# An encoder kernel in split fp32: the last three steps of each down product by tiles, and projections, seam and end reordered

## The chip, the cores and the metric

The kernel runs on one core of one Trainium2 chip. The metric is the device time of one execution in microseconds (us), first to last instruction and what lies around them. A core has TensorE (PE, matmuls into eight PSUM banks), VectorE (DVE), ScalarE (ACT), GpSimd (POOL), and SyncE (SP), which here only issues transfers. Each engine runs its own instruction list in order and waits on semaphores for the others.

## What is computed

Two independent sequences (x_prompt and x_sample) of 1024 tokens and 1024 channels go through the same layer, all in float32:

```python
h = rmsnorm(x, norm_mix)
z = h @ w_in
a = pool_mixer(z[..., :512]) @ w_up_pool          # means over 2, 4, 8, 16 tokens, small maps
b = attention_branch(z[..., 512:]) @ w_up_attn    # 12 heads, three dilated windows, merged
gates = sigmoid(h @ w_gate + b_gate)
x = x + (g_a * a + g_b * b) @ w_out
h = rmsnorm(x, norm_ffn)
x = x + (silu(h @ w_ffn_gate) * (h @ w_ffn_up)) @ w_ffn_down   # 2816 hidden channels
y = rmsnorm(x, norm_final)
```

## The kernel before

**Split operands.** Each float32 operand is held as a high part (rounded by ACT) and a low part (the rest, subtracted by POOL or DVE). A product is three matmuls: high by high, high by low, low by high (`three`, L1089 to L1093). A group of three matmuls of 128x512 is the unit of TensorE's work here.

**Seven products in place of eight.** The large products are done by a Strassen-Winograd scheme of seven products on half-size blocks, with sums and differences of the blocks formed by POOL.

**The down product.** The last large product of a sequence (hidden activations by `w_ffn_down`) is seven down products, numbered o = 0 to 6 (`DOWN`, L59). Each is KC = 11 steps (k = 0 to 10), and each step takes one 128-row piece of the contraction. In a step TensorE does four groups, one for each tile t = 0 to 3 of 128 tokens; each tile has its own PSUM bank (`down_products`, L1357). So a down product is 44 groups, and the four banks are complete one after another in its last step. Products use bank group 0 or 1 in turn; products 0, 1, 5 and 6 begin with cleared banks and the others go on adding.

For a step with index m the other engines make two operands.

- ACT rounds the activations (`part_hi`, L1672, tile d_hi) and then the weights (`operand_hi`, L1461, tile t_hi). It does both for step m + 4 after step m of TensorE is done, since there are four slots of each (RING = 4). "Step done" is the semaphore `prod_done`, which the last matmul of tile t = 3 raises.
- DVE subtracts d_lo (`part_low`, L2132).
- POOL subtracts t_lo (`low_part`, L836). In products 1, 2 and 4 POOL first forms the weights' difference for the next step, and in product 5 it forms, behind t_lo, the difference for product 6 (`rows_sum`, L956, L977): two POOL instructions a step, where products 0, 3 and 6 have one.
- SP loads the activations from DRAM (d_rows) and the weights (w_ffn_down).

DVE then adds the four banks into X, the residual (`add_quarter`, L2139), at the first step of the next product. The results of product 4 are added twice, the second time at (5, 1). Where steps are written (o, k), o is the down product and k its step.

**The seam.** While sequence 0 is in its down products, the first normalisation of sequence 1 is made in between: SP loads the tokens after step (3, 0), ACT makes their statistics (`first_stats`, at (2, 10), (3, 2), (5, 1), (6, 9)), DVE normalises (`first_norm`, at (3, 0), (3, 2), (3, 5), (3, 7), (5, 4), (5, 6), and two at (6, 10)), and POOL forms four sums for each pair p of token tiles (`mix_s1` to `mix_s4`, one at each place of `SUMS_AT`, L136). In product 6 TensorE transposes the parts between its steps (`part_transposes`, `EARLY`, L131), ACT and DVE copy them out, and ACT and DVE also make the final norm of the first four tiles of sequence 0 (`final_stats`, `final_norm`), which SP stores. Behind those stores SP loads the last tokens and the first weights of sequence 1.

**Up and out projections.** Before the up projections DVE splits the four pooled operands (`mix_low`, L2080), the fourth behind the loop over the front products, so behind `after_product` of the last gate product (L1929, which writes gst when SP's earlier store of it has landed). The up projections (`up_products`) fill banks 4r to 4r + 3 for channel block j, r = j mod 2, and DVE multiplies the gates in (`gated`, L2087, L2094). Then `out_products` (L1336) does 24 visits in three rounds; a visit adds one 128-row block of `w_out` into the banks of two or three token tiles. Visit 0 takes tiles 0, 1, 2, that is banks 0 to 5, and banks 4 and 5 are those that the gates of block j = 7 are read from.

**The end.** In sequence 1 DVE adds the four tiles of product 6, ACT makes the statistics of the last four tiles, DVE normalises them, and ACT issues their four stores, behind all four statistics (`store_out`, L1690).

## Time and profile before

| what | us |
|---|---|
| median of three runs | 2621.22 (2619.81 to 2622.74) |
| the profiled execution, its own time | 2620.28 |
| its span, first to last instruction | 2618.5 |
| TensorE busy | 2543.1 (97% of the span), 12048 matmuls |
| POOL, DVE, ACT busy | 1874.5, 1221.4, 1051.9 |
| mean granted clock of TensorE | 0.995 |

A busy time is the union of an engine's instructions. Matmuls are pipelined, so their records overlap, and a step in which TensorE waits a little for each operand can still look fully busy: the length of a product is read from the starts of its first matmuls, not from the busy share. "Idle" in a row is the time that the engine stood before that instruction, with what released it. A row of the view of stretches gives start and end, the length, then for PE, PEld (weight loads), DVE, ACT and POOL the busy time and, in brackets, the count of instructions, then TensorE's granted clock as a share of full speed, the DMA share and GB/s; the stretches below run from the first matmul of one down product to the first of the next. A row of the timeline gives start, length, engine, line, operation, tiles and shapes.

### The profile page before, as it was taken

How to read it: one execution, taken by the hardware profiler on the slowest of the kernel's cores; microseconds unless marked ns; L12 is line 12 of the kernel's file. 1: busy time of each engine (PE TensorE's matmuls, PEld its weight loads, DVE VectorE, ACT ScalarE, POOL GpSimd, SP SyncE). 2: the span in 40 equal slices, each digit the busy share in tenths (PEclk: the TensorE clock that was granted, in tenths of full speed). 3: DMA queues.
4: the chain of work that ended last, by engine and by line, in shares of the span. 5: the costliest groups of instructions: out<-in, count | busy, mean ns of one | idle time of the engine just before them, and what ended most of it. 6: DMA issues, size and time to landing. Idle time of an engine off the chain costs nothing. (4 is left out here: it accounts for less than half of the span.)

```text
span 2618.5 us, 33338 instructions
## 1 busy us (share of the span) xinstructions
PE 2543.1 (97%) x12048; PEld 2065.2 (79%) x12048; DVE 1221.4 (47%) x1673; ACT 1051.9 (40%) x2034; POOL 1874.5 (72%) x1376
## 2 busy tenths in 40 slices
PE   6999999999999999998989999999999999999998
PEld 5887777778888888876778877777878888888786
DVE  6753556644322222354677535566443222223545
ACT  5224554444433233344552345544444333233444
POOL 7775456545888888797977754465468888887985
PEclk8999999999999999999999999999999999999999
DMA  3444455462233333463444435554623333335534
GB/s 130 128 131 125 144 158 175 143 243 77 81 108 97 116 98 97 157 206 120 141 141 124 149 107 154 152 175 161 229 81 92 97 99 107 101 105 165 181 122 140
DMA packets 331858, 350.76 MB, mean 134 GB/s; under 512 B 30640, under 2 KB 242992, under 8 KB 330160
## 3 DMA queue, kind: packets, MB, share of 16 engines
q1 hardware_dynamic: 329392, 342.23, 41.6%
q10 hardware_dynamic: 2304, 6.40, 0.7%
q8 instruction: 98, 1.61, 0.3%
q14 instruction: 64, 0.52, 0.1%
HBM read 249.28 MB, written 99.29 MB: 133 GB/s over the span
## 5 line engine op out<-in xcount | busy, mean ns | idle before, releaser
L1091 PE MATMUL ps<-S,t_hi 128*128 128x512 f32 (+2 forms) x2336 | 917.1, 393 | 9.1 <-POOL t_lo L841 6.3
L1093 PE MATMUL ps<-S,t_lo 128*128 128x512 f32 (+2 forms) x2336 | 903.7, 387 | 0.0
L1092 PE MATMUL ps<-S,t_hi 128*128 128x512 f32 (+2 forms) x2336 | 903.0, 387 | 0.0
L1091 PEld LDWEIGHTS ps<-S,t_hi 128*128 128x128 f32 x2336 | 438.7, 188 | 110.3 <-issue 12.7
L1093 PEld LDWEIGHTS ps<-S,t_lo 128*128 128x128 f32 x2336 | 438.6, 188 | 89.9
L1092 PEld LDWEIGHTS ps<-S,t_hi 128*128 128x128 f32 x2336 | 439.1, 188 | 84.1
L841 POOL TENSOR_TENSOR t_lo<-wraw,t_hi 128x512 fp32r<-128x512 f32 x185 | 246.4, 1332 | 205.8 <-ACT t_hi L1489 203.4
L841 POOL TENSOR_TENSOR t_lo<-wraw_ff,t_hi 128x512 fp32r<-128x512 f32 x225 | 293.9, 1307 | 93.4 <-ACT t_hi L1489 89.3
L1489 ACT CAST t_hi<-wraw_ff 128x512 fp32r<-128x512 f32 x225 | 139.6, 623 | 366.8 <-PE ps L1093 366.6
L2136 DVE TENSOR_TENSOR d_lo<-d_raw,d_hi 128x512 fp32r<-128x512 f32 x154 | 178.9, 1164 | 207.0 <-ACT d_hi L1680 206.4
L841 POOL TENSOR_TENSOR t_lo<-R,t_hi 128x512 fp32r<-128x512 f32 x154 | 233.1, 1519 | 46.5 <-ACT t_hi L1489 46.5
L1091 PE MATMUL ps<-t_hi,d_hi 128*128 128x512 f32 x616 | 248.7, 404 | 11.8 <-POOL t_lo L841 11.8
L1092 PE MATMUL ps<-t_lo,d_hi 128*128 128x512 f32 x616 | 241.1, 391 | 0.0
L1093 PE MATMUL ps<-t_hi,d_lo 128*128 128x512 f32 x616 | 241.1, 391 | 0.0
L1489 ACT CAST t_hi<-wraw 128x512 fp32r<-128x512 f32 x185 | 115.2, 623 | 303.7 <-PE ps L1093 299.0
L1919 DVE TENSOR_TENSOR u<-u,ps 128x512 f32<-128x512 f32 x82 | 56.3, 686 | 255.8 <-PE ps L1093 255.8
L841 POOL TENSOR_TENSOR t_lo<-t,t_hi 128x512 fp32r<-128x512 f32 x74 | 101.7, 1374 | 98.6 <-ACT t_hi L1489 98.3
L1091 PEld LDWEIGHTS ps<-t_hi,d_hi 128*128 128x128 f32 x616 | 116.3, 189 | 54.8 <-POOL t_lo L841 32.3
L1680 ACT CAST d_hi<-d_raw 128x512 fp32r<-128x512 f32 x154 | 95.3, 619 | 137.0 <-PE ps L1093 93.7
L995 POOL TENSOR_TENSOR wo_lo<-wo_raw,wo_hi 128x1024 fp32r<-128x1024 f32 x32 | 82.5, 2582 | 91.8 <-ACT wo_hi L1646 91.8
L1922 DVE TENSOR_TENSOR v<-u,ps 128x512 f32<-128x512 f32 x82 | 56.4, 687 | 195.8 <-PE ps L1093 195.7
L1489 ACT CAST t_hi<-R 128x512 fp32r<-128x512 f32 x154 | 95.3, 619 | 116.5 <-POOL R L977 101.8
(169 smaller groups left out, 4054.6 us busy)
## 6 DMA issues: line engine op xcount, KB each, us to landing
d_raw<-d_rows SPq DMA_DIRECT2D x154, 256.0 KB, 3.2
d_rows<-act_f SPq DMA_DIRECT2D x110, 256.0 KB, 2.1
wraw_ff<-w_ffn_up SPq DMA_DIRECT2D x44, 512.0 KB, 4.7
R<-w_ffn_down SPq DMA_DIRECT2D x88, 256.0 KB, 3.1
wraw<-w_in SPq DMA_DIRECT2D x42, 512.0 KB, 5.6
sp_rows<-gst SPq DMA_DIRECT2D x80, 256.0 KB, 2.5
wraw_ff<-w_ffn_gate SPq DMA_DIRECT2D x40, 512.0 KB, 5.0
wo_raw<-w_out SPq DMA_DIRECT2D x36, 512.0 KB, 3.3
```

The costliest lines, as they stand in the source:

```text
L841: nc.gpsimd.tensor_tensor(shape(t_lo[r][:, :]), src, shape(t_hi[r][:, :]).bitcast(F32), ALU.subtract).then_inc(t_ready, 1)
L995: nc.gpsimd.tensor_tensor(wo_lo[r][:, :], wo_raw[op % 2][:, :], wo_hi[r][:, :].bitcast(F32), ALU.subtract).then_inc(wo_ready, 1)
L1091: nc.tensor.matmul(o_ps, w[0], r[0], start=begins, stop=False, skip_group_check=True)
L1092: nc.tensor.matmul(o_ps, w[0], r[1], start=False, stop=False, skip_group_check=True)
L1093: return nc.tensor.matmul(o_ps, w[1], r[0], start=False, stop=ends, skip_group_check=True)
L1489: nc.scalar.copy(dst, src).then_inc(thi_ready, 1)
L1680: nc.scalar.copy(d_hi[d % 4][:, :], d_raw[d % 4][:, :]).then_inc(dhi_ready, 1)
L1919: V_.tensor_tensor(u, u, b1, ALU.add).then_inc(sums_done, 1)
L1922: V_.tensor_tensor(v1[:, :], u, b2, ALU.add).then_inc(sums_done, 1)
L2136: V_.tensor_tensor(d_lo[d % 4][:, :], d_raw[d % 4][:, :], d_hi[d % 4][:, :].bitcast(F32), ALU.subtract).then_inc(d_ready, 1)
```

## The change

Four parts, with the diff below.

- **Tail.** In every down product but product 6 of sequence 0, TensorE does steps 0 to 7 as before and then goes tile by tile: steps 8, 9, 10 for tile 0, then for tiles 1, 2 and 3. The order of the 44 groups changes, not their number. DVE adds tiles 0 to 2 at step 8 of the same product and tile 3 at step 0 of the next.
- **Seam.** The sums, statistics and norms for sequence 1 sit at other steps: the second pair's sums all in product 6, the third pair's statistics, norms and sums later in product 6, with its last two sums behind POOL's last down step. The four final norms of product 6 sit one step later.
- **Projections.** The fourth `mix_low` goes ahead of the last `after_product`. `out_products` takes tiles 0 and 1 of visits 0 and 1 first, and then tile 2 of both.
- **End.** In sequence 1 DVE adds tiles 0 and 1, normalises, adds tile 2, normalises, adds tile 3, and normalises twice. SP issues all eight stores of sequence 1, each when its tile is ready.

```diff
@@ -120,6 +120,8 @@
         VISITS.append((_r, _k, _op))
 N_WO = len(SLOT_OF)
 
+FIRST_VISITS = ((0, (0, 1)), (1, (0, 1)), (0, (2,)), (1, (2,)))
+
 N2_AFTER = {8 + v: [v - 1] for v in range(1, 8)}
 N2_AFTER.update({17: [7, 8], 18: [9, 10], 19: [11, 12], 20: [13, 14]})
 
@@ -133,7 +135,11 @@
 EARLY_DONE = 21
 
 
-SUMS_AT = ((3, 3), (3, 4), (3, 5), (3, 6), (3, 8), (3, 9), (6, 0), (6, 1), (6, 5), (6, 6), (6, 7), (6, 8))
+
+SUMS_AT = ((3, 6), (3, 7), (3, 8), (3, 9), (6, 0), (6, 1), (6, 2), (6, 3), (6, 9), (6, 10))
+
+
+TAIL = 3
 
 
 
@@ -781,7 +787,7 @@
                     if m == N_PROD + 3 * KC and s + 1 < SEQS:
                         sp.wait_ge(prod_done, due("prod_done", s, N_PROD))
                         first_tokens(s + 1)
-                for n in range(2 if s + 1 < SEQS else 4):
+                for n in range(2 if s + 1 < SEQS else TT):
                     store_out(s, n)
 
 
@@ -1068,6 +1074,8 @@
                             mix_s3(s + 1, 0, p)
                         else:
                             mix_s4(s + 1, 0, p)
+                    if s + 1 < SEQS and m == N_OPS - 1:
+                        mix_last(s + 1, 0, 2)
                     i = FF_PAIRS // 2 - 1
                     if m == N_PROD + 3:
                         first_sums(s, i)
@@ -1354,14 +1362,14 @@
                 if v < 7 and t == OUT_ROUNDS[rnd][0][-1]:
                     ins.then_inc(wo_used, 1)
 
-            def down_products(s, m):
+            def down_products(s, m, ts=range(4)):
 
                 o, k = divmod(m - N_PROD, KC)
                 part, group, begins, _ = DOWN[o]
                 pe.wait_ge(t_ready, due("t_ready", s, m + 1))
                 pe.wait_ge(d_ready, due("d_ready", s, m - N_PROD + 1))
                 slot, d = slot_of(m), (m - N_PROD) % 4
-                for t in range(4):
+                for t in ts:
                     b = 4 * group + t
                     if k == 0:
                         bank_read(b)
@@ -1393,7 +1401,9 @@
                     pair_banks(s, n)
                 for j, a in UP_ORDER:
                     up_products(s, j, a)
-                for visit in range(len(VISITS) - 3):
+                for visit, tiles in FIRST_VISITS:
+                    out_products(s, visit, tiles)
+                for visit in range(2, len(VISITS) - 3):
                     out_products(s, visit, OUT_ROUNDS[visit // 8][0])
                     part_transposes(s, 1, N2_AFTER.get(visit, ()))
                 for t in OUT_ROUNDS[-1][0]:
@@ -1405,11 +1415,17 @@
                     for m in range(7 * n + (4 if n == FF0 else 0), 7 * n + 7):
                         pair_product(s, m)
                     pair_banks(s, n)
-                for m in range(N_PROD, N_OPS):
-                    down_products(s, m)
-                    o, k = divmod(m - N_PROD, KC)
-                    if o == 6 and s + 1 < SEQS:
-                        part_transposes(s + 1, 0, EARLY.get(k, ()))
+                for o in range(len(DOWN)):
+                    first = N_PROD + KC * o
+                    seam = o == 6 and s + 1 < SEQS
+                    for k in range(KC if seam else KC - TAIL):
+                        down_products(s, first + k)
+                        if seam:
+                            part_transposes(s + 1, 0, EARLY.get(k, ()))
+                    if not seam:
+                        for t in range(4):
+                            for k in range(KC - TAIL, KC):
+                                down_products(s, first + k, (t,))
 
         @block.scalar
         def _(act):
@@ -1824,12 +1840,12 @@
                     if o == 2 and k == 0:
                         act.wait_ge(ff_stored[0], due("ff_stored0", s, 36))
                         act.dma_start(g_fin[:, :], norm_final.partition_broadcast(P)).then_inc(gfin_in, 16)
-                    if s + 1 < SEQS and (o, k) in ((2, 10), (3, 2), (5, 1)):
-                        first_stats(s + 1, ((2, 10), (3, 2), (5, 1)).index((o, k)))
+                    if s + 1 < SEQS and (o, k) in ((2, 10), (3, 2), (6, 0)):
+                        first_stats(s + 1, ((2, 10), (3, 2), (6, 0)).index((o, k)))
                     if o == 6 and s + 1 < SEQS:
                         part_his(s + 1, 0, EARLY.get(k - 1, ()))
-                    if o == 6 and k in (1, 2, 5, 6):
-                        final_stats(s, (1, 2, 5, 6).index(k))
+                    if o == 6 and k in (2, 3, 6, 7):
+                        final_stats(s, (2, 3, 6, 7).index(k))
                     if o == 6 and k == 9 and s + 1 < SEQS:
                         first_stats(s + 1, 3)
                 if s + 1 < SEQS:
@@ -1837,8 +1853,6 @@
                 else:
                     for n in range(4, TT):
                         final_stats(s, n)
-                    for n in range(4, TT):
-                        store_out(s, n)
 
             for q in range(4):
                 act.wait_ge(tiles_stored[q], due(f"tiles_stored{q}", SEQS, 0))
@@ -2136,11 +2150,11 @@
                 V_.tensor_tensor(d_lo[d % 4][:, :], d_raw[d % 4][:, :], d_hi[d % 4][:, :].bitcast(F32), ALU.subtract
                                  ).then_inc(d_ready, 1)
 
-            def add_quarter(s, o, which):
+            def add_quarter(s, o, which, ts=range(4)):
 
                 _, group, _, quarters = DOWN[o]
                 h, n = quarters[which]
-                for t in range(4):
+                for t in ts:
                     if t == 3:
                         dve.wait_ge(prod_done, due("prod_done", s, N_PROD + KC * (o + 1)))
                     else:
@@ -2171,6 +2185,8 @@
                 dve.wait_ge(const_in, 16 * 4)
 
                 for m in range(FRONT + 1):
+                    if m == FRONT:
+                        mix_low(s, 3)
                     if m:
                         after_product(s, m - 1)
                     n, o = divmod(m - 1, 7)
@@ -2202,7 +2218,6 @@
                         merge_step(s, 2 * (m - SPREAD0 - 1) + 1)
                     if MERGE0 + 12 <= m < MERGE0 + 15:
                         mix_low(s, m - MERGE0 - 12)
-                mix_low(s, 3)
                 merged_low(s, 0)
                 merged_low(s, 1)
                 for j in range(TT):
@@ -2239,17 +2254,19 @@
                 for m in range(N_PROD, N_OPS):
                     o, k = divmod(m - N_PROD, KC)
                     if k == 0 and o:
-                        add_quarter(s, o - 1, 0)
+                        add_quarter(s, o - 1, 0, (3,))
+                    if k == KC - TAIL and o < 6:
+                        add_quarter(s, o, 0, range(3))
                     if k == 1 and o == 5:
                         add_quarter(s, o - 1, 1)
                     if m + 4 < N_OPS:
                         part_low(s, m + 4)
                     if o == 6 and k == 2:
                         dve.wait_ge(gfin_in, due("gfin_in", s, 1))
-                    if s + 1 < SEQS and (o, k) in ((3, 0), (3, 2), (3, 5), (3, 7), (5, 4), (5, 6)):
-                        first_norm(s + 1, ((3, 0), (3, 2), (3, 5), (3, 7), (5, 4), (5, 6)).index((o, k)))
-                    if o == 6 and k in (2, 3, 6, 7):
-                        final_norm(s, (2, 3, 6, 7).index(k))
+                    if s + 1 < SEQS and (o, k) in ((3, 0), (3, 1), (3, 4), (3, 6), (6, 1), (6, 2)):
+                        first_norm(s + 1, ((3, 0), (3, 1), (3, 4), (3, 6), (6, 1), (6, 2)).index((o, k)))
+                    if o == 6 and k in (3, 4, 7, 8):
+                        final_norm(s, (3, 4, 7, 8).index(k))
                     if o == 6 and s + 1 < SEQS:
                         part_los(s + 1, 0, EARLY.get(k - 1, ()))
                     if o == 6 and k == 10 and s + 1 < SEQS:
@@ -2257,15 +2274,18 @@
                         first_norm(s + 1, 7)
                 if s + 1 < SEQS:
                     part_los(s + 1, 0, EARLY[KC - 1])
-                add_quarter(s, 6, 0)
                 if s + 1 < SEQS:
+                    add_quarter(s, 6, 0)
                     part_los(s + 1, 0, range(EARLY_DONE, 24))
                     final_norm(s, 4)
                     final_norm(s, 5)
                     part_los(s + 1, 0, range(24, 28))
                 else:
-                    for n in range(4, TT):
-                        final_norm(s, n)
+                    add_quarter(s, 6, 0, (0, 1))
+                    for t in range(4):
+                        final_norm(s, 4 + t)
+                        if t < 2:
+                            add_quarter(s, 6, 0, (t + 2,))
 
 
 def constants():
```

## Rows read from the trace of the kernel before

**Rows 1.** Who waited for whom, TensorE only: us in total, times, longest.

```profile
PE ps L1091 <- POOL t_lo L841: 18.1, 18, 4.5
...
PE ps L1091 <- DVE mix_lo L2084: 4.0, 2, 2.5
PE ps L1091 <- DVE gl L2094: 3.6, 2, 2.2
```

**Rows 2.** Stretches (columns: see above), down products 1, 2, 3, 5 and 6 of sequence 0.

```profile
1121.65:1153.11 31.46, 31.46 (x134) 24.08 (x132) 16.43 (x15) 12.58 (x22) 31.46 (x23) 1.00 0.56 183
1153.11:1185.31 32.20, 32.20 (x133) 24.18 (x133) 14.64 (x14) 10.91 (x19) 29.51 (x20) 1.00 0.77 266
1185.31:1227.63 42.32, 32.75 (x133) 25.40 (x131) 20.78 (x25) 20.34 (x38) 25.96 (x20) 0.96 0.28 84
...
1259.83:1292.65 32.82, 31.21 (x134) 24.28 (x132) 24.95 (x24) 15.98 (x30) 32.82 (x22) 1.00 0.50 158
1292.65:1337.65 45.00, 41.11 (x209) 33.58 (x209) 30.24 (x41) 26.78 (x53) 24.97 (x17) 0.96 0.42 134
```

**Rows 3.** The same for down products 1 and 5 of sequence 1.

```profile
2423.45:2455.38 31.93, 31.93 (x133) 23.94 (x131) 17.90 (x16) 12.60 (x22) 31.93 (x23) 1.00 0.55 182
...
2547.43:2577.35 29.92, 29.92 (x133) 24.78 (x132) 15.97 (x19) 12.57 (x22) 29.92 (x21) 1.00 0.47 153
```

**Rows 4.** Timeline, POOL, last step of down product 0, sequence 1.

```profile
2416.38 1.75 POOL L977 TENSOR_TENSOR R<-R,R 128x512 f32<-128x512 f32 x1
2418.10 1.74 POOL L841 TENSOR_TENSOR t_lo<-R,t_hi 128x512 fp32r<-128x512 f32 x1
```

**Rows 5.** Timeline, ACT, the two casts of one down step.

```profile
2409.87 0.62 ACT L1680 CAST d_hi<-d_raw 128x512 fp32r<-128x512 f32 x1 [3.98 <-DMA d_raw<-d_rows]
2410.40 0.61 ACT L1489 CAST t_hi<-R 128x512 fp32r<-128x512 f32 x1
```

**Rows 6.** Stretches, TensorE only, right after its longest wait in down product 3.

```profile
1202.80:1207.17 4.37, 4.37 (x12) 0.63 0.17 56
1202.66:1206.07 3.41, 3.27 (x8) 0.50 0.24 73
```

**Rows 7.** Timeline, POOL, its first sum for the next sequence, down product 3.

```profile
1199.82 1.26 POOL L809 TENSOR_TENSOR mixed<-xb 128x512 f32<-128x512 f32 x1 [6.66 <-DVE xb L1869]
```

**Rows 8.** Timeline, ACT, the fourth pooled operand's high part, sequence 0.

```profile
490.45 1.05 ACT L1615 CAST mix_hi<-ml 128x1024 fp32r<-128x1024 f32 x1 [0.68 <-DMA ml<-mix_rows]
```

**Rows 9.** Timeline, DVE, the pooled operands' low parts, sequence 0.

```profile
491.84 1.63 DVE L2084 TENSOR_TENSOR mix_lo<-ml,mix_hi 128x1024 fp32r<-128x1024 f32 x1
495.37 0.69 DVE L1929 TENSOR_TENSOR gst<-u,ps 128x512 f32<-128x512 f32 x1 [1.89 <-DMA sp_rows<-gst]
495.97 1.22 DVE L2084 TENSOR_TENSOR mix_lo<-ml,mix_hi 128x1024 fp32r<-128x1024 f32 x1
```

**Rows 10.** Timeline, DVE, last gate tile of sequence 0.

```profile
564.99 2.47 DVE L2094 TENSOR_TENSOR gl<-gl,ps 128x512 f32<-128x512 f32 x4
```

**Rows 11.** Timeline, POOL, first weight pair of sequence 1.

```profile
1332.05 1.31 POOL L879 TENSOR_TENSOR t_ff<-wraw_ff 128x512 f32<-128x512 f32 x1 [8.07 <-DMA wraw_ff<-w_in]
1340.09 1.28 POOL L841 TENSOR_TENSOR t_lo<-wraw_ff,t_hi 128x512 fp32r<-128x512 f32 x1 [6.73 <-ACT t_hi L1489]
```

**Rows 12.** Timeline, DVE, end of the program.

```profile
2605.43 2.73 DVE L2151 TENSOR_TENSOR X<-X,ps 128x512 f32<-128x512 f32 x4 [3.80 <-PE ps L1093]
...
2612.45 1.28 DVE L1859 SCALAR_TENSOR_TENSOR X<-X,rstd,g_fin 128x1024 f32<-128x1024 f32 x1
```

**Rows 13.** Timeline, ACT, last tile's statistics.

```profile
2610.27 1.04 ACT L1426 ACTIVATE squares<-X 128x1024 f32<-128x1024 f32 x1
...
2611.44 0.29 ACT L1428 ACTIVATE std<-ss,eps 128x1 f32<-128x1 f32 x1
```

**Rows 14.** Stores of the output, 2600 to 2619 us.

```profile
DMA to landing us min/median/max: 2.7/3.2/4.3
```

**Rows 15.** Stores of the output issued by SP, 2585 to 2605 us.

```profile
DMA to landing us min/median/max: 2.6/2.7/3.4
```

## The prediction

> **What bounds the kernel now.** I read who waited for whom first. TensorE, busy nearly throughout, waits openly for little: 18.1 us for POOL's low parts, 4.0 for `mix_lo`, 3.6 for the gates [rows 1]. It never shows a wait for DVE's additions into X, so moving these gives nothing by itself inside a sequence. Then the stretches product by product. A down product that nothing holds takes 29.92 us, which is 44 groups of 0.68, or 11 steps of 2.72 [rows 3]. Product 1 of either sequence takes 31.5 or 31.9 with POOL busy all the time [rows 2, 3]: POOL, not TensorE, sets its pace. One POOL instruction takes 1.25 us, and 1.75 where it meets a DVE subtraction [rows 4, 7, 11], so two a step and one such meeting make 2.95 us, over TensorE's 2.72. In products 4 and 5 of sequence 1 this costs nothing (29.92, product 4 is the same), although POOL never rests there: it can stand up to four steps ahead, and over 22 steps spends 22 x 0.23 = 5 us of that lead [rows 3]. The operands' lead is what the tail changes. In sequence 0, product 3 takes 42.32, that is 12.4 over the free length: POOL stood 6.66 us for a norm ahead of its first sum, with its low parts queued behind [rows 2, 7].
>
> **Tail: the cost.** TensorE wants step 9's operands 0.68 us after the start of step 8 and step 10's after 1.36, where it wanted them after 2.72 and 5.44. And `prod_done` of step 8 comes two groups (1.36) before the end of the product in place of 5.44 before, so for most of the tail POOL has nothing released to do, however long its lead.
> - Product 0, sequence 1. Step 10's low part ends at 2419.84 [rows 4]. The product ends at 2423.45 [rows 3], so step 8 began 8.16 earlier, at 2415.29, and the new order wants it at 2416.65: 3.2 us late. I take the same for sequence 0: 6.4 together.
> - Products with two POOL instructions. Let X be the end of the previous product. Its step 8 frees its slots at X - 1.36; with about 0.35 of hand-overs, the two casts (1.14 [rows 5]) and POOL's 1.3, the next product's step 1 is ready at X + 1.4. Nine more steps at 2.95 put step 10 at X + 28.0. Behind it TensorE still has ten groups, 6.8 us, so the product takes 34.8. In 2 and 4 one difference fewer stands in this queue: 33.55.
> - Against before: product 1, 34.8 - 31.46 = 3.3 and 34.8 - 31.93 = 2.9; product 2, 33.55 - 32.20 = 1.35, the same in both sequences; product 4, 1.35 in sequence 0 (it took as long as product 2) and 33.55 - 29.92 = 3.6; product 5, 34.8 - 32.82 = 2.0 and 34.8 - 29.92 = 4.9 [rows 2, 3]. Sum 20.7.
> - Product 3 of sequence 1 and the last product have one POOL instruction a step: nothing.
> So the tail costs 27.1. Bounds: zero beyond the first 6.4 if POOL should have its lead all the same; 3 more if DVE's instructions meet POOL's more often (0.5 each).
>
> **Slow clock behind long waits.** After a wait of 4.5 us in product 3 the granted clock was 0.50, the lower level, 1.2 GHz, and the step took 4.37 in place of 2.72 [rows 1, 6]: 1.65 more. The tails of products 1 and 5 have two waits of some 2.3 us, 0.68 apart, as does product 3's in sequence 0. I charge 1.65 to three of these five, +5.0; bounds 0 and every tail with a wait, 10 x 1.65 = 16.5. The Trainium skill ("TensorE: Matmul & The Clock Gate", section on HAM oscillation in real kernels) says that a kernel whose tiles each end in a wait falls to the slow clock again and again; by that rule the upper bound holds, and it is a rival below. The trace has one such wait per product at most, and can't decide.
>
> **Seam.** In product 3 POOL no longer waits early. Its first sum can start where the norm lets it, as now 14.5 after the product's start (1199.82 - 1185.31 [rows 2, 7]), but four sums, four low parts and a first difference, nine instructions at 1.25, now stand ahead of step 10's operand, with four DVE subtractions (0.45 each) and two norms (1.28 each, the length in rows 12): 15.6. Operand at 30.1, product at 36.9 against 42.32: -5.4. Bounds -12.4 and 0. Product 6 (45.0, against 29.92 and 21 transposed parts) changes its waits: two first norms come in at (6, 1) and (6, 2), and the four final norms sit one step later. I take 0, bounds -4 and +8 (two steps of 3.6). Behind it, token and weight loads of sequence 1 go out one step, 3.6, later: now the pair sum waits for its weights until 1332.05, but its low part only starts at 1340.09, held by ACT [rows 11]. Cover 6.7, cost 0; if it were gone, up to 3.6. POOL's last two sums go behind its last low part, which it makes up to four steps ahead of TensorE, and their transposes are the very last: 0, at worst two sums, 2.5.
>
> **Projections.** The fourth high part is ready at 491.50, the third low part ends at 493.47, but DVE then stands for a store and adds until 495.97 [rows 8, 9]. Moved ahead, the low part ends at 494.7, when TensorE wants it (its wait of 2.5 ended at 497.2). Both waits go: -4.0 [rows 1]. Behind it queue the addition, its store and the gates' loads; these wait for a store that lands at 495.37 anyhow. At the gates, tile 2 of visit 0 waits for DVE's multiplication of 564.99 [rows 10]. Four groups (2.72) of visit 1 go ahead and its second low part is ready, so both waits go: -3.6 [rows 1]. The third and fourth weights of `w_out` come 0.4 later, under visits of 4.1. Sum -7.7; bounds 0 and -7.7, as nothing else can be gained there.
>
> **End.** Now the last addition starts when TensorE ends (2607.48 = E), four norms follow, and the last ends at 2613.73, E + 6.25 [rows 12]. Then: the casts for step 10 are released at E - 10.9, and behind them (1.14) ACT makes two statistics (1.46 each [rows 13]) by E - 6.8, so the norms at steps 7 and 8 (1.4 each) hold DVE until E - 5.3; additions 0 and 1 by E - 3.4, norm, addition 2 by E - 1.1, norm until E + 0.35, addition 3 (0.68), statistics 1.46 [rows 13], norm 1.4: E + 3.95. That is -2.3. The last of ACT's stores took up to 4.3 us to land, SP's 2.6 to 3.4 [rows 14, 15], and stores now leave 1.5 to 2 apart: -1.3. Sum -3.6, bounds -2.3 and -5.
>
> **Sum.** 27.1 + 5.0 - 5.4 - 7.7 - 3.6 = +15.4 on the profiled execution's 2620.28 (1.8 of it outside its span, unchanged): 2635.7. The median before is 0.9 higher: 2636.6, say 2636.5. A measurement of this kernel can tell about 0.2% (5.2 us) from no change.
>
> **Rivals.**
> - **POOL's lead survives (faster).** If the casts and low parts of the tail's steps are mostly ready when TensorE turns to tile 0, only the first tails cost (6.4), and product 3 loses its full 12.4: 2621.2 + 6.4 - 12.4 - 7.7 - 3.6 = 2603.9. For it: products 4 and 5 of sequence 1 hid POOL fully. Against: slots are released by tile 3 alone. It decides the sign once tails and slow clock cost under 23.7 in place of my 32.1 plus the 7.0 in product 3's own tail. 0.07.
> - **The slow clock at every tail.** +11.5: 2648. For it the skill's rule, against it that waits of 1.6 and 2.7 us in product 3 brought no lower clock. 0.15.
> - **The seam stalls.** Norms of 1.28 and POOL's sums crowd (6, 1) to (6, 4), and product 6 gives back 4 to 8: 2641 to 2645. 0.10.
> - **Gains and costs cancel.** Tails at half my price, the rest as summed: 2623. 0.08.
>
> **Numbers.** My forecast has 0.60. Slower by over 0.2%: 0.60 + 0.15 + 0.10 = 0.85 less a little for a forecast that misses by 10, 0.84. Within: 0.09. Faster: 0.07. Range 2625 to 2649: from the forecast with no slow clock and tails a quarter cheaper (-5, -7), to the slow clock everywhere.
>
> **What would show it.** Down product 1 near 34.8, 2 and 4 near 33.5, 5 near 34.8, in both sequences, and in each TensorE idle ahead of steps 9 and 10 of tile 0, released by POOL's t_lo, with POOL idle just before, released by ACT; sequence 1's product 3 at 29.9. Waits for `mix_lo` and gates gone; last norm 4 us behind the last matmul. Wrong if product 5 of sequence 1 is still near 30, or if TensorE's wait for t_lo stays near 18 in total (I expect some 45).

## The result, and the profile after

The changed kernel takes **2658.89 us** (median of four, 2658.24 to 2660.98) against 2620.72 for the kernel before beside it: ratio 1.0146, 95% interval 1.0128 to 1.0163, so 38 us slower. I had forecast slower, 2636.5, and a range that ended at 2649. The direction was right and the size less than half. The profiled execution took 2658.24, its span 2656.4, with a mean granted clock of 0.986 (before 0.995).

Who waited for whom, TensorE only (beside [rows 1]):

```profile
PE ps L1099 <- POOL t_lo L847: 41.4, 32, 4.1
...
PE ps L1099 <- DVE v L1936: 5.5, 3, 4.4
```

The wait for POOL's low parts went from 18.1 to 41.4, near the 45 that I expected. The waits for `mix_lo` and for the gates are gone from the list. A wait for `v` is new.

Stretches of the down products, from first matmul to first matmul (columns: us, then busy us and count of PE, PEld, DVE, ACT, POOL, granted clock, DMA share, GB/s): products 1, 2, 3, 5, 6 of sequence 0, then 0, 1, 3, 4, 5 of sequence 1 (beside [rows 2, 3]).

```profile
1121.09:1158.31 37.22, 33.87 (x133) 25.82 (x132) 17.47 (x16) 12.46 (x24) 31.92 (x22) 0.91 0.47 156
1158.31:1193.19 34.88, 32.92 (x133) 25.15 (x132) 17.16 (x16) 12.47 (x24) 28.24 (x19) 0.95 0.70 249
1193.19:1232.41 39.22, 33.29 (x133) 26.68 (x132) 26.70 (x24) 18.79 (x37) 29.43 (x18) 0.87 0.24 74
1267.67:1304.98 37.31, 33.59 (x134) 25.95 (x132) 17.91 (x20) 12.27 (x24) 31.94 (x22) 0.91 0.38 120
1304.98:1353.21 48.23, 42.66 (x209) 34.94 (x208) 35.77 (x44) 30.13 (x62) 28.22 (x18) 0.93 0.40 131
2411.45:2444.96 33.51, 30.81 (x133) 24.54 (x132) 13.00 (x17) 11.48 (x21) 22.03 (x16) 1.00 0.69 228
2444.96:2482.46 37.50, 33.77 (x134) 25.80 (x132) 17.35 (x16) 12.57 (x24) 31.94 (x22) 0.91 0.47 154
2517.48:2547.40 29.92, 29.92 (x133) 24.77 (x132) 13.13 (x16) 12.37 (x24) 19.84 (x14) 1.00 0.33 97
2547.40:2582.36 34.96, 32.90 (x134) 25.21 (x132) 17.48 (x16) 12.38 (x24) 29.47 (x20) 0.95 0.40 121
2582.36:2619.32 36.96, 32.92 (x133) 25.46 (x132) 18.13 (x20) 12.36 (x24) 30.73 (x21) 0.95 0.38 121
```

Read the clock column beside the first. In these rows every product that grew has a clock under 1.00, but for product 0 of sequence 1, which grew by 3.1 (from 30.42) at 1.00; product 3 of sequence 1, with one POOL instruction a step, neither grew nor lost the clock. Product 1 took 37.2 and 37.5 where I had said 34.8.

One tail, product 1 of sequence 1. POOL's timeline:

```profile
2467.45 1.28 POOL L983 TENSOR_TENSOR R<-R,R 128x512 f32<-128x512 f32 x1
2468.70 1.71 POOL L847 TENSOR_TENSOR t_lo<-R,t_hi 128x512 fp32r<-128x512 f32 x1
2470.37 1.72 POOL L983 TENSOR_TENSOR R<-R,R 128x512 f32<-128x512 f32 x1
2472.05 1.26 POOL L847 TENSOR_TENSOR t_lo<-R,t_hi 128x512 fp32r<-128x512 f32 x1
...
2482.57 1.30 POOL L847 TENSOR_TENSOR t_lo<-R,t_hi 128x512 fp32r<-128x512 f32 x1 [5.56 <-ACT t_hi L1505]
```

And TensorE's:

```profile
2468.12 0.40 PE L1101 MATMUL ps<-t_hi,d_lo 128*128 128x512 f32 x1
2470.46 0.51 PE L1099 MATMUL ps<-t_hi,d_hi 128*128 128x512 f32 x1 [1.95 <-POOL t_lo L847]
...
2473.36 0.80 PE L1099 MATMUL ps<-t_hi,d_hi 128*128 128x512 f32 x1 [1.78 <-POOL t_lo L847]
2473.96 0.63 PE L1100 MATMUL ps<-t_lo,d_hi 128*128 128x512 f32 x1
```

POOL runs without a break up to step 10's low part, which ends at 2473.31, 28.35 after the product's start, where I had worked out 28.0. After three more instructions it stands 5.56, until the tail's slots are released and ACT has rounded again. I had named as a sign that POOL would be idle just before TensorE's waits; its idle time lies behind them, at the product's end. TensorE waits 1.95, works one group, waits 1.78, where I had said some 2.3 twice. In lengths this is the forecast. Then look at the durations: behind the second wait a matmul takes 0.63 in place of 0.40. The ten groups left cost 9.1 us, not 6.8.

Stretches with the clock (same columns): four slow ones, the second of which lies behind the wait for `v`, and then the stretch behind the first tail of sequence 1 and that behind the first tail of sequence 0.

```profile
1218.43:1228.67 10.24, 6.11 (x15) 4.74 (x15) 3.00 (x4) 0.62 (x1) 7.91 (x6) 0.50 0.08 30
1767.97:1771.39 3.42, 3.42 (x10) 2.68 (x9) 3.35 (x7) 0.10 (x1) 1.28 (x1) 0.50 0.20 77
2471.12:2477.95 6.83, 5.05 (x13) 3.62 (x12) 0.69 (x1) 0.62 (x1) 5.89 (x5) 0.50 0.62 192
2508.67:2512.08 3.41, 3.23 (x9) 2.32 (x8) 1.70 (x2) 0.00 (x0) 2.14 (x2) 0.50 0.25 77
...
2438.00:2441.00 3.00, 2.98 (x13) 2.48 (x14) 0.69 (x1) 0.00 (x0) 3.00 (x3) 1.00 0.60 198
1112.62:1116.03 3.41, 3.41 (x8) 2.74 (x9) 0.69 (x1) 0.00 (x0) 3.41 (x3) 0.50 0.51 172
```

Eleven tails waited (products 0 to 5 of sequence 0; 0, 1, 2, 4, 5 of sequence 1), and ten of them show the lower level, 1.2 GHz. Apart from the program's start and end, the trace of before has two such stretches and this one thirteen. In product 1 above the clock fell at 2471.12, so behind the first wait and ahead of the second.

The end, DVE (beside [rows 12]): TensorE ends at 2649.4, the last norm at 2653.29, 3.9 later, where I had worked out 3.95; before it was 6.25.

```profile
2649.59 0.68 DVE L2165 TENSOR_TENSOR X<-X,ps 128x512 f32<-128x512 f32 x1
...
2652.01 1.28 DVE L1873 SCALAR_TENSOR_TENSOR X<-X,rstd,g_fin 128x1024 f32<-128x1024 f32 x1
```

**The wait for `v`** in sequence 1's front is one that I had not foreseen. DVE of the kernel after, where it adds a pooled job's neighbours:

```profile
1758.09 0.07 DVE L2005 MEMSET Uh<- 128x8 f32 x1 [3.06 <-DMA Uh<-sp_rows]
1758.19 0.71 DVE L2009 TENSOR_TENSOR pw<-Uh 128x527 f32<-128x527 f32 x1
1758.93 5.08 DVE L2009 TENSOR_TENSOR pw<-pw 128x525 f32<-128x525 f32 x3
```

The same of the kernel before:

```profile
1740.69 0.07 DVE L1991 MEMSET Uh<- 128x8 f32 x1 [1.16 <-DMA Uh<-sp_rows]
...
1741.53 2.18 DVE L1995 TENSOR_TENSOR pw<-pw 128x525 f32<-128x525 f32 x3
```

The load landed 1.9 later against DVE's work (DVE stood 3.06 before it, in place of 1.16). The three additions then fell on POOL's instructions, which run back to back from 1758.55, and took 5.08 in place of 2.18. `v`, queued behind, came late, TensorE waited 4.40, and the clock fell (1767.97 above).

What SP, of the kernel after, waited for ahead of this load (4.1 before):

```profile
SPq L565 <- DMA mix_rows<-Uh: 4.9, 1, 4.9
```

The program issues this load only when the store of the pooled job before it has landed. Against DVE's instruction on `u` ahead of the additions, that store was issued 0.7 later than in the kernel before, it took 0.8 more from there to the load's issue (5.84 against 5.08), and the load took 0.5 more to land (3.30 against 2.84): that makes the 1.9.

### The profile page after: what moved, and what is told of

Same layout as the page of the kernel before. It is cut to its first block and busy times, and to the rows that moved or that the text cites. A ratio compares the mean times of both kernels' runs of the same rounds, so it can differ in the third digit from the quotient of the medians.

```text
span 2656.4 us, 33459 instructions
## 1 busy us (share of the span) xinstructions
PE 2564.8 (97%) x12048; PEld 2080.4 (78%) x12048; DVE 1235.8 (47%) x1673; ACT 1050.5 (40%) x2034; POOL 1873.5 (71%) x1376
## 5 line engine op out<-in xcount | busy, mean ns | idle before, releaser
L1099 PE MATMUL ps<-t_hi,d_hi 128*128 128x512 f32 x616 | 256.1, 416 | 35.2 <-POOL t_lo L847 35.0
L2150 DVE TENSOR_TENSOR d_lo<-d_raw,d_hi 128x512 fp32r<-128x512 f32 x154 | 188.6, 1233 | 162.0 <-ACT d_hi L1696 160.8
L1101 PE MATMUL ps<-t_hi,d_lo 128*128 128x512 f32 x616 | 248.5, 403 | 0.0
L1100 PE MATMUL ps<-t_lo,d_hi 128*128 128x512 f32 x616 | 248.3, 403 | 0.0
L1101 PEld LDWEIGHTS ps<-t_hi,d_lo 128*128 128x128 f32 x616 | 120.6, 196 | 27.0
```

What stands on the lines that cost most here:

```text
L1099: nc.tensor.matmul(o_ps, w[0], r[0], start=begins, stop=False, skip_group_check=True)
L1100: nc.tensor.matmul(o_ps, w[0], r[1], start=False, stop=False, skip_group_check=True)
L1101: return nc.tensor.matmul(o_ps, w[1], r[0], start=False, stop=ends, skip_group_check=True)
L2150: V_.tensor_tensor(d_lo[d % 4][:, :], d_raw[d % 4][:, :], d_hi[d % 4][:, :].bitcast(F32), ALU.subtract).then_inc(d_ready, 1)
```

## The experiments

A ratio is always to the kernel before, run beside. Product lengths are stretches as above. The kernel before took 2620.72 beside the changed kernel and 2620.64 to 2622.77 beside the experiments, so a difference between an experiment and the changed kernel can be up to 2 us larger than their medians say. Product 6 of sequence 0 is measured from here on to 0.16 behind the start of the transposes that follow it: so it took 45.30 in the kernel before (the row in [rows 2] ends 0.30 earlier) and 48.40 in the changed one (the row above ends 0.17 earlier).

### 1. The tail in the last product only

```diff
-                    for k in range(KC if seam else KC - TAIL):
+                    tail = o == 6 and not seam
+                    for k in range(KC - TAIL if tail else KC):
...
-                    if not seam:
+                    if tail:
...
-                        add_quarter(s, o - 1, 0, (3,))
-                    if k == KC - TAIL and o < 6:
-                        add_quarter(s, o, 0, range(3))
+                        add_quarter(s, o - 1, 0)
```

> The changed kernel with the order by tiles left only in the last product of sequence 1; every other product again takes its eleven steps with all four tiles, and DVE adds all four tiles at the next product's step 0. Projections, seam and end stay as the change has them. Theory (the tails and the slow clock that they bring are the whole loss): the projections' 5.8 and the end's 4.1 stay gained, product 3 of sequence 0 falls to about 32 (10 less than before), the front of sequence 1 stays 3 over before or loses that too: 2595 to 2606, products 4 and 5 of sequence 1 back at 29.92, no slow clock but one or two stretches. Rival (the moved work of projections and seam costs a good part of the 38): over 2612, with product 6 and the front of sequence 1 still long.

Measured: **2604.18 us**, ratio 0.9923 (0.9908 to 0.9938). Stretches, products 3 and 6 of sequence 0, then 1 and 5 of sequence 1:

```profile
1181.31:1216.82 35.51, 31.21 (x133) 24.28 (x131) 28.67 (x25) 20.25 (x38) 28.73 (x18) 1.00 0.34 99
1279.91:1326.92 47.01, 41.19 (x211) 33.87 (x211) 35.31 (x45) 29.14 (x59) 28.98 (x19) 0.96 0.41 128
2409.19:2440.75 31.56, 31.56 (x133) 24.04 (x131) 17.61 (x16) 12.57 (x22) 31.56 (x23) 1.00 0.57 184
2532.82:2562.74 29.92, 29.92 (x134) 24.77 (x132) 15.97 (x19) 12.56 (x22) 29.92 (x21) 1.00 0.47 153
```

The theory holds: without the tails the change saves 18.6 us on the kernel before, so the tails and what they bring cost 54.7 (56.8 with either kernel taken against the one beside it). Product 3 came to 35.5, not the 32 that I had put in. Product 6 is 1.7 longer than before. TensorE waits 0.61 for `v` here.

### 2. The order by tiles alone

The kernel before with the loop of the change's TensorE part (its lines from `for o in range(len(DOWN))` on, TAIL = 3) and nothing else.

> The kernel before with the order by tiles alone, in every product but product 6 of sequence 0; DVE's additions, sums, norms, projections and end as they were. Theory (tails and their slow clock): all products as long as in the changed kernel (35.9, 37.2, 34.9, 35.3, 37.3), product 3 of sequence 0 some 5 to 8 over its 42.3, and none of the gains: 2664 to 2675. Rival (the tails by themselves cost what I had forecast, 27 and 5, and the rest of the loss is from what was moved): about 2653. Clock at the lower level ahead of step 9 and 10 in nearly every product by the theory, in at most five by the rival.

Measured: **2687.39 us**, ratio 1.0239 (1.0224 to 1.0254). Stretches, product 1 of sequence 1 and product 3 of sequence 0:

```profile
2468.85:2506.69 37.84, 33.97 (x134) 26.01 (x132) 16.12 (x16) 12.46 (x24) 31.99 (x22) 0.91 0.48 153
1202.46:1248.14 45.68, 35.70 (x134) 27.96 (x132) 18.18 (x24) 18.78 (x37) 26.62 (x20) 0.85 0.22 63
```

Worse than either theory said, 12 over the upper end of the first: 64.6 over the kernel before. Product 1 is that of the changed kernel (37.84 against 37.50), although DVE adds where it did before, so the early additions aren't what makes it long. Four other products came out 1.9 to 2.3 longer than in the changed kernel (2 and 5 of sequence 0, 0 and 4 of sequence 1), three of them with 3.4 us more at the lower clock; whether the later additions have a part in that, this run doesn't show. What came on top: product 3 of sequence 0, 45.7 against 39.2, TensorE's waits for `mix_lo` and the gates, 9.8 in all against 7.6 before, 2.98 for `v`, and 13.7 us at the lower clock in the two fronts (the program's start apart), where the changed kernel has 3.4.

### 3. A tail of two steps

```diff
-TAIL = 3
+TAIL = 2
```

> The changed kernel with a tail of two steps in place of three. The tail's first step then is step 9, step 10's operands are wanted 0.68 later, and nine steps free their slots in the old order. Theory (the price is that of POOL's released work: step 8's slots are freed at the end of the product less 5.4 + 1.4 in place of less 1.4): a product with two POOL instructions takes about 32.5 in place of 37, two thirds to all of the 38 comes back, 2600 to 2625, with few stretches of slow clock. Rival (what costs is that a tail asks for its operands at all in quick succession): each product gives back a third at most, 2640 to 2650.

Measured: **2611.50 us**, ratio 0.9951 (0.9935 to 0.9966). Stretches, products 1, 2, 5 of sequence 1, and TensorE at the tail of the first:

```profile
2412.77:2445.15 32.38, 30.43 (x134) 24.60 (x132) 16.76 (x15) 12.65 (x23) 32.38 (x23) 1.00 0.55 179
2445.15:2475.91 30.76, 30.48 (x133) 24.54 (x132) 16.81 (x15) 12.66 (x23) 29.21 (x20) 1.00 0.58 180
2535.77:2566.98 31.21, 30.22 (x133) 24.70 (x132) 17.67 (x19) 12.47 (x23) 30.15 (x21) 1.00 0.49 153
...
2440.25 0.50 PE L1099 MATMUL ps<-t_hi,d_hi 128*128 128x512 f32 x1 [1.95 <-POOL t_lo L847]
```

One step less in the tail gives back 47 of the 54.7; of the 7.3 left, product 3 of sequence 0 holds 2.3 (37.85 against 35.52) and the wait for `v` 2.8. The tail still asks for the last step's operands 0.68 after the one before, so this asking by itself is not what costs, and the rival falls. What differs is how many steps' slots come free together at the very end, and how much earlier than before step 10 is wanted (by the order of the groups 2.04 in place of 4.08); this run alone can't part the two. Product 1 still has a wait of 1.95, in both sequences, and keeps the clock at 1.00. Products 1 and 2 take 63.1 together here and 63.8 with no tail (31.56 and 32.23): what the one takes longer, the other gives back.

### 4. TensorE kept busy in the waits

Beside these lines, the edit makes the tile of zeros and has TensorE wait for it once, at the start.

```diff
+                                if t == 0 and k > 8 and (o in (0, 1, 2, 4, 5) or (s == 0 and o == 3)):
+                                    for _ in range(7 if k == 9 else 4):
+                                        nc.tensor.matmul(ps[0:32, 4 * DOWN[o][1], :], zero[:, :],
+                                                         t_hi[slot_of(first + 8)][:, :], start=False, stop=False,
+                                                         skip_group_check=True)
```

> The changed kernel with TensorE kept busy in the waits of the tails: seven matmuls by a 32-column tile of zeros ahead of step 9 of tile 0 and four ahead of step 10, in products 0, 1, 2, 4, 5 of both sequences and product 3 of sequence 0 (they add zeros to the same sum). They need nothing that isn't there, and take about 1.5 to 1.9 and 0.9 to 1.1. Theory (the part of the loss that I missed is the clock, about 15 to 20 in all): the granted clock stays at 1.00 through the down products, the waits are as long as before less the filling, 2638 to 2644. Rival (POOL's pace alone sets the product's length, and the slow stretches lie in its shadow): no difference, or up to 8 slower where the filling holds up the step.

Measured: **2639.71 us**, ratio 1.0064 (1.0047 to 1.0080): 19.2 less than the changed kernel, for 121 more matmuls that add zeros. Stretches, products 1, 2, 4, 5 of sequence 1:

```profile
2428.66:2464.06 35.40, 34.02 (x145) 25.42 (x143) 17.57 (x16) 12.47 (x24) 32.04 (x22) 1.00 0.51 164
2464.06:2498.15 34.09, 33.73 (x144) 25.50 (x143) 17.52 (x16) 12.36 (x24) 28.30 (x19) 1.00 0.46 147
2528.07:2562.16 34.09, 33.75 (x144) 25.50 (x143) 17.57 (x16) 12.36 (x24) 29.57 (x20) 1.00 0.40 124
2562.16:2597.66 35.50, 33.96 (x144) 25.55 (x143) 17.29 (x20) 12.36 (x24) 30.89 (x21) 1.00 0.39 126
```

TensorE at a tail, where seven fillers take 1.79 and leave a wait of 0.34:

```profile
2452.06 1.79 PE L1435 MATMUL ps<-t_hi,zero 128*32 128x512 f32 x7
2454.19 0.50 PE L1104 MATMUL ps<-t_hi,d_hi 128*128 128x512 f32 x1 [0.34 <-POOL t_lo L851]
```

The clock is 1.00 in all four products (of the eleven filled tails only product 3's, with a wait of 3.23 left, fell to 0.50, for 3.4 us), and they are within 0.7 of my forecast lengths (34.8, 33.55, 33.55, 34.8). The waiting is still there, filled; what went is the slow clock behind it. In the down products of both sequences the difference to the changed kernel is 15.8 us; the other 6 of the spans' 21.6 lie in sequence 1's front, where the wait for `v` was 0.60 this time, which the fillers in the tails don't explain.

### 5 and 6. POOL's differences of the weights cut short

In both, after and before (most of the weights' differences are left out, so these two serve for the time alone):

```diff
-                nc.gpsimd.tensor_tensor(a, b, c, ALU.subtract).then_inc(t_made, 1)
+                nc.gpsimd.tensor_tensor(a[:, 0:8], b[:, 0:8], c[:, 0:8], ALU.subtract).then_inc(t_made, 1)
```

> The changed kernel with POOL's differences of the down weights (the second POOL instruction of a step, in products 1, 2, 4, 5) cut to 8 of 512 columns; it leaves out most of the weights' differences. Theory (a tail costs what POOL must still do between the release of step 8's slots and step 10: ten steps at 2.95 with two full instructions, at 2.72 or less with one): products 1, 2, 4, 5 of sequence 1 fall from 37.5, 35.0, 35.0, 37.0 to 30 to 33.5, that is, what is left is the hand-over at the tail's end as in product 0 (33.5) at most; 2628 to 2642. Rival (the asking for three steps in a row costs the same whatever POOL does): they stay within 1 of what they were, 2650 or more.

> The kernel before with the same differences cut to 8 columns, as the base for the last one; it leaves out the same. Products 1, 2 and 5 of sequence 0 and 1 and 2 of sequence 1 fall from 31 to 33 to 29.9 to 30.5: some 9 less, about 2612. Product 3 of sequence 0 keeps its wait for the norm (39 to 42). With the theory of POOL's pace the changed kernel stands at most 20 over this one (three quarters of it the tails of single-instruction kind, 3.6 each at most), against 38 between the two full kernels; the rival has 38 here as well.

Measured: **2599.74** (ratio 0.9910, 0.9896 to 0.9925) and **2607.95** (0.9943, 0.9923 to 0.9963). Stretches of the changed kernel so cut, products 0 and 1 of sequence 1:

```profile
2377.58:2409.32 31.74, 30.66 (x134) 24.55 (x133) 13.99 (x17) 11.49 (x21) 19.19 (x16) 1.00 0.74 240
2409.32:2439.24 29.92, 29.92 (x134) 24.78 (x133) 11.44 (x16) 12.57 (x24) 17.70 (x22) 1.00 0.60 194
```

With one POOL instruction a step nearly gone, three-step tails cost nothing: products 1, 2, 4, 5 take 29.92, tail and all, at clock 1.00, and the changed kernel turns from 38 slower into 8.2 faster than its base. My own theory was too cautious here: it left up to 3.6 a product, and its range, 2628 to 2642, ended 28 above the result. In these products it is POOL's second instruction that makes the tail expensive. Product 0, which has one in its last steps alone ([rows 4]), takes 31.7, against 33.5 in the changed kernel and 30.4 before.

### 7. The projections alone

With `FIRST_VISITS` as in the diff of the change:

```diff
-                for visit in range(len(VISITS) - 3):
+                for visit, tiles in FIRST_VISITS:
+                    out_products(s, visit, tiles)
+                for visit in range(2, len(VISITS) - 3):
...
+                    if m == FRONT:
+                        mix_low(s, 3)
...
-                mix_low(s, 3)
```

> The kernel before with the reordered projections alone: mix_low(s, 3) ahead of product FRONT's work on DVE, and the first visits to w_out by two tiles. As forecast: -7.7 (both waits for mix_lo and both for the gates gone), 2613. By what the changed kernel shows: 5.8 in sequence 0, and in sequence 1 the same unless the wait of 4.4 for a pooled job's sums comes with it: -5 to -8 without that wait, about 0 to -2 with it. The wait stays away by the theory that it is a matter of how late one load happens to land, and comes by the rival that the moved work causes it.

Measured: **2612.07 us**, ratio 0.9955 (0.9940 to 0.9970): 10.2 faster, a little over the 7.7 that I had forecast. (Of its span's 9.2, 6.0 lie ahead of sequence 0's down products, 2.4 from product 6 of sequence 0 to sequence 1's down products, and 1.1 in product 3, which the edit doesn't touch.) Both pairs of waits are gone, and TensorE waits 0.69 for `v`. So the moved work alone doesn't cause that wait. It came in the changed kernel and in experiments 2, 3 and 5 (4.40, 2.98, 2.79, 2.68), and not in before, 1, 4, 6, 7, 8, 9 and 10 (all under 0.9). The traces of all twelve kernels tell the rest. From the issue of the store of the pooled job before to the issue of the load it took 5.82 to 6.25 in the four that wait and 4.86 to 5.22 in the eight that don't; DVE stood 2.28 to 3.06 for the load in the four and 1.16 to 1.65 in the eight; and the three additions took 5.08 in the changed kernel, 4.12 in experiments 2, 3 and 5, and 2.17 to 3.24 in the rest.

### 8. The seam alone

The positions of `SUMS_AT`, of the first and final statistics and norms, and `mix_last` behind the last low part, as in the diff of the change, on the kernel before.

> The kernel before with the seam alone: positions of first sums, first norms, first and final statistics and final norms; the down products keep their order and additions, projections and end stay. Theory (from the changed kernel with the tail left only in the last product, where product 3 took 35.5 and product 6 some 47.0): product 3 of sequence 0 falls by 6 to 7, product 6 rises by 1 to 2, 2616 to 2618. Rival (the two first norms moved to product 6 cost more when nothing else has moved): product 6 at 49 or over, 2620 or more.

Measured: **2616.95 us**, ratio 0.9975 (0.9963 to 0.9987). Stretches, products 3 and 6 of sequence 0:

```profile
1187.45:1222.28 34.83, 31.19 (x133) 24.28 (x131) 27.93 (x25) 20.35 (x38) 28.46 (x18) 1.00 0.34 103
1285.41:1332.70 47.29, 41.80 (x211) 33.79 (x211) 35.46 (x45) 29.16 (x59) 28.58 (x19) 0.96 0.40 127
```

Product 3 gives 7.5, product 6 takes back 2.0. Projections 10.2 and seam 5.3 make 15.5 of the 18.6 of experiment 1; the 3.1 left are near the end's 4.0, which I did not run by itself.

### 9. Three additions a step earlier, without the tail

On experiment 1:

```diff
-                        add_quarter(s, o - 1, 0)
+                        add_quarter(s, o - 1, 0, (3,))
+                    if k == KC - 1 and o < 6:
+                        add_quarter(s, o, 0, range(3))
```

> The changed kernel with its tail only in the last product of sequence 1, as in the first experiment, and with DVE's additions of tiles 0 to 2 at step 10 in place of the next product's step 0 (a tile's last product is step 10's group, so they can start there). With the tail of two steps, products 2 (both sequences) and 4 (sequence 0) took 30.8, 30.8 and 29.9, against 32.2 with no tail. Theory (that is from the additions, which no longer stand ahead of DVE's low parts at step 0 or meet POOL there): products 2 fall to 30.5 to 31.3, product 4 of sequence 0 to about 30, in all 4 to 5 less than the first experiment, 2599 to 2601. Rival (it came from the order of the products alone, or the additions now hold up DVE at step 10): no difference or up to 3 slower, 2604 to 2607.

Measured: **2602.78 us**, ratio 0.9930 (0.9916 to 0.9943), no difference from experiment 1 that can be measured. Product 2 stays at 32.2 and 32.1. My theory falls, and of the readings of product 2's 30.8 in experiment 3 the one given there is left: product 1's longer time handed on.

### 10. The two first norms back in product 5

On experiment 9:

```diff
-                    if s + 1 < SEQS and (o, k) in ((2, 10), (3, 2), (6, 0)):
-                        first_stats(s + 1, ((2, 10), (3, 2), (6, 0)).index((o, k)))
+                    if s + 1 < SEQS and (o, k) in ((2, 10), (3, 2), (5, 1)):
+                        first_stats(s + 1, ((2, 10), (3, 2), (5, 1)).index((o, k)))
...
-                    if s + 1 < SEQS and (o, k) in ((3, 0), (3, 1), (3, 4), (3, 6), (6, 1), (6, 2)):
-                        first_norm(s + 1, ((3, 0), (3, 1), (3, 4), (3, 6), (6, 1), (6, 2)).index((o, k)))
+                    if s + 1 < SEQS and (o, k) in ((3, 0), (3, 1), (3, 4), (3, 6), (5, 4), (5, 6)):
+                        first_norm(s + 1, ((3, 0), (3, 1), (3, 4), (3, 6), (5, 4), (5, 6)).index((o, k)))
```

> The last one with the two first norms and their statistics, which the change moved to product 6, back in product 5 of sequence 0. Theory (they are what makes product 6 take 47.0 in place of 45.1): product 6 falls by 1 to 2, product 5 rises by at most 1: 0 to 2 under the last one. Rival (product 6 is longer by the order of POOL's sums and the final norms, one step later): product 6 stays at 46.5 to 47, product 5 rises as before (32.8 in place of 30.9), 1 to 2 over the last one.

Measured: **2602.41 us**, ratio 0.9923 (0.9911 to 0.9935). Stretches, products 5 and 6 of sequence 0:

```profile
1249.93:1282.68 32.75, 31.18 (x134) 24.29 (x132) 25.88 (x27) 15.95 (x30) 32.75 (x22) 1.00 0.45 155
1282.68:1327.60 44.92, 41.56 (x211) 33.75 (x211) 29.40 (x39) 26.58 (x53) 27.25 (x19) 0.96 0.42 134
```

Product 6 falls by 2.1 against experiment 1, so the norms are what made it longer, as the theory had it; product 5 rises by 1.9, as the rival had it, where the theory allowed 1. The two norms with their statistics cost about 2 in either place. Experiments 1, 9 and 10 can't be told apart and beat both kernels, by some 0.75% before and 2% after.

## Why the prediction was right in direction and wrong in size

Each term against what the spans show (37.9 between them). "Without the clock" is experiment 4's product less the kernel before's (in products 3 and 6 of sequence 0 both of these have one slow stretch of 3.4 us); the clock's own line is the changed kernel's down products less experiment 4's.

| Term | Forecast | Measured |
|---|---|---|
| Tails of ten products, without the clock | +27.1 | +31.7 |
| Slow clock behind waits | +5.0 | +15.8 |
| Product 3 of sequence 0, without the clock | -5.4 | -4.2 |
| Product 6 of sequence 0, without the clock | 0 | +1.5 |
| Projections and sequence 1's front | -7.7 | -2.8 |
| End | -3.6 | -4.0 |
| Sum | +15.4 | +38.0 |

**The step that failed** is "I charge 1.65 to three of these five, +5.0", together with the words that stood in for evidence, "waits of 1.6 and 2.7 us in product 3 brought no lower clock". Those were single waits in one product of the kernel before, and they say little about waits that come in every product, two of them 0.68 apart. Ten of eleven tails fell to 1.2 GHz, single waits of 1.95 among them (2508.67 above). The size of one was about right, 1.65 forecast and 14.1 over the eleven tails (the other 1.7 of the line is product 6's); the count was wrong. I had that number on the page as an upper bound, 16.5, and had given the rival that reaches it 0.15. Of the 22.6 between the sums, 10.8 are this line, 4.9 sequence 1's front, 4.6 the tails' lengths, 1.5 product 6 and 1.2 product 3; the end gave 0.4 more than forecast. What decides whether a wait is followed by the lower clock stays open: experiment 3's product 1 waited the same 1.95 and kept 1.00. The Trainium skill ("TensorE: Matmul & The Clock Gate", HAM oscillation in real kernels) tells of a kernel that waits some 3 to 5 us after every tile and falls to the slow clock every time. The prediction took that for a rule on the waits here, which are shorter; the page doesn't say so much. The trace shows the fall for waits of 1.9 to 4.1 in ten of eleven tails.

**Tails.** The mechanism stands, shown by experiments 3 and 5: slots of three steps released at the end, two POOL instructions a step, no lead left. The lengths of products 1, 2, 4 and 5 were 0.5 to 0.7 short, which experiment 4's fillers may partly be: product 0 of sequence 1 saw no slow clock in the changed kernel and took 33.5 there, and 33.9 with fillers. Against the rival that POOL's lead survives, product 5 of sequence 1 took 36.96, not 30.

**Projections.** The term itself was sound (experiment 7: 10.2). In the changed kernel sequence 0 gained 5.8, but sequence 1's front came out 3.0 longer than before. Of that the wait for `v` is 4.4 and the slow stretch behind it some 1.7; with both away, in experiment 1, the same front took 1051.8 against 1055.1 before. The 1.7 is an estimate: half of the stretch's 3.42. I had named no such rival: my costs for gone cover looked at what the moved work delays, not at how a load that lands 1.9 later puts three additions beside POOL's instructions. Most of the lateness comes with the store that the load must wait for (above); why it lands later in some kernels is open. The transfers around it are the same ones; no run varied them.

**Seam.** Product 3 was forecast at 36.9 and came to 39.2; with fillers, which left it one slow stretch of 3.4 us, to 38.2. Without a tail it takes 35.5 (experiment 1). That product 6 would change by nothing was wrong by 1.5 to 2, inside its bounds (-4 to +8); experiment 10 names the two first norms.

**End.** Right to 0.4, by the working given.

**The range** ended at the one rival's 2649, as if the slow clock, dearer tails and a stall in the seam excluded each other. Nothing makes them exclude each other: the clock came nearly in full (+10.8), the tails beyond their bound (+4.6 against +3), and the seam in small part (product 6, +1.5). Stacked, the bounds stated (+11.5 clock, +3 tails, +8 seam) reach 2659; that the result lies just there is chance, as the parts differ and 4.9 of it came from sequence 1's front.

## What to carry to other kernels

Before steps are regrouped so that one tile finishes early, ask which buffers are released by the last tile, and whether the engine that refills them has any slack: here it needed 2.95 us a step against TensorE's 2.72, and three steps released together left it no lead. Price the clock with the waits: here a tail's waits cost TensorE some 1.4 us more than they lasted, and filling them with matmuls by zeros gave 15.8 us back in the down products, zeros included. When the bounds of several terms can occur together, the range must add them.

## What the runs showed of the hardware that I had not expected

- The lower clock does not follow from a wait's length alone. A wait of 2.39 at 1110.19 was followed by 0.50, the same wait of 2.39 at 2435.63 by 1.00 (the last two stretches of the clock's fence); in the eight us before, TensorE had also stood 0.96 in the first case and 0.30 in the second; no run shows whether that decides it. A wait of 1.95 was followed by 0.50 in products 2 and 4 of the changed kernel and by 1.00 in product 1 of experiment 3.

```profile
1112.58 0.79 PE L1099 MATMUL ps<-t_hi,d_hi 128*128 128x512 f32 x1 [2.39 <-POOL t_lo L847]
...
2438.02 0.50 PE L1099 MATMUL ps<-t_hi,d_hi 128*128 128x512 f32 x1 [2.39 <-POOL t_lo L847]
```

- DVE loses more than half its pace beside POOL: an addition of 128x525 took 0.73 nearly alone (2.18 for three) and 1.69 beside it (5.08), while POOL's 1.26 became 1.71. The Trainium skill ("SBUF — State Buffer", SBUF: two separate sides) says that the pair of ports they share is held for a whole instruction and the other engine stands still. The trace agrees as far as it goes: an addition then lasts as long as a POOL instruction (1.69 and 1.71). But alone the two take 0.73 and 1.26, 1.99 together, so in part they did run at the same time, or one of the figures holds more than the time at the ports; the trace can't tell.
- A load 1.9 us late grew to a wait of 4.4 us on TensorE and a slow clock: the three additions lost another 2.90 by that meeting, and DVE's work behind them took as long as before.
